# Four small reorderings around a full TensorE: residual copies, a pass change, operand places, and the last stores

## The reference

```python
h = xn @ w_up                       # 1024 -> 2 * 2816
hc = conv_b + sum_j shift(h, j) * conv_w[j]   # causal, 3 taps, per channel
gate, up = split(hc); y = (silu(gate) * up) @ w_down   # 2816 -> 1024
h = h + y
out = h * rsqrt(mean(h * h) + 1e-6) * final_g
```

## Time and profile before

| | |
|---|---|
| median of 3 runs | 1462.41 us (1461.9 to 1462.45) |
| the profiled execution's own time | 1460.3 us |
| its span, first to last instruction | 1458.4 us |
| PE busy | 1443.6 us, 99% |
| DVE busy | 1012.1 us, 69% |
| ACT busy | 700.6 us, 48% |
| POOL busy | 47.4 us, 3% |
| mean granted TensorE clock | 0.998 |

### The profile page before, as it was taken

The page is one execution under the profiler, slowest core; times in us unless marked ns, Lnnn a source line. Parts: engine busy times, 40 slices in busy tenths (PEclk is TensorE's granted clock), DMA queues, the critical chain, the costliest instruction groups (busy, mean ns, idle before and its releaser), DMA issues.

```text
span 1458.4 us, 19919 instructions
## 1 busy us (share of the span) xinstructions
PE 1443.6 (99%) x6983; PEld 1192.4 (82%) x6983; DVE 1012.1 (69%) x1710; ACT 700.6 (48%) x1200; POOL 47.4 (3%) x35
## 2 busy tenths in 40 slices
PE   9999999999999999999999999999999999999997
PEld 7888888888888888888888888888887888888876
DVE  7877667655777734776477776675656888888976
ACT  7655555434444422443475555553344343344665
POOL 0000000002100000000200000000020000000002
PEclk9999999999999999999999999999999999999999
DMA  6222212232322233222432222222333655555554
GB/s 250 87 73 88 87 58 74 87 102 72 130 94 93 79 98 112 101 95 72 131 121 89 86 73 80 65 80 88 122 130 116 206 180 190 211 178 186 203 166 144
DMA packets 49434, 171.38 MB, mean 118 GB/s; under 512 B 6465, under 2 KB 6593, under 8 KB 46289
## 3 DMA queue, kind: packets, MB, share of 16 engines
q1 hardware_dynamic: 45760, 147.43, 30.8%
q10 hardware_dynamic: 3600, 22.99, 4.2%
HBM read 156.70 MB, written 13.63 MB: 117 GB/s over the span
## 4 chain that ended last, share of the span: by engine, by line
PE 93%; DVE 3%; ACT 2%; DMA 1%; issue 1%; POOL 0%; SPq 0%; POOLq 0%; ACTq 0%; DVEq 0%
PE dense L784 26%; PE dense L786 26%; PE dense L785 26%; PE turned L867 2%; PE branch L894 1%; PE dense L799 1%; PE dense L801 1%; PE dense L800 1%; PE dense L1049 1%; PE dense L1051 1%; PE dense L1050 1%; PE scores L859 1%; DMA raw<-in_w_last 1%; PE scores L856 1%; PE branch L880 1%
## 5 line engine op out<-in xcount | busy, mean ns | idle before, releaser
L784 PE MATMUL dense<-hg,whi 128*128 128x512 f32 x1304 | 516.6, 396 | 3.7 <-DVE wlo L1540 3.5
L786 PE MATMUL dense<-hg,wlo 128*128 128x512 f32 x1304 | 508.9, 390 | 0.0
L785 PE MATMUL dense<-hg,whi 128*128 128x512 f32 x1304 | 508.4, 390 | 0.0
L1118 ACT ACTIVATE whi<-raw 128x1024 fp32r<-128x1024 f32 (+3 forms) x242 | 240.8, 995 | 427.2 <-PE dense L786 421.1
L1540 DVE TENSOR_TENSOR wlo<-raw,whi 128x1024 fp32r<-128x1024 f32 (+3 forms) x242 | 276.9, 1144 | 117.0 <-ACT whi L1118 115.0
L784 PEld LDWEIGHTS dense<-hg,whi 128*128 128x128 f32 x1304 | 245.5, 188 | 56.4 <-issue 5.0
L786 PEld LDWEIGHTS dense<-hg,wlo 128*128 128x128 f32 x1304 | 244.9, 188 | 52.1
L785 PEld LDWEIGHTS dense<-hg,whi 128*128 128x128 f32 x1304 | 245.3, 188 | 48.0 <-issue 0.2
L784 PE MATMUL dense<-act,whi 128*128 128x512 f32 x432 | 170.0, 394 | 0.5 <-DVE wlo L1540 0.5
L786 PE MATMUL dense<-act,wlo 128*128 128x512 f32 x432 | 168.4, 390 | 0.0
L785 PE MATMUL dense<-act,whi 128*128 128x512 f32 x432 | 168.3, 390 | 0.0
(11 more groups left out here) (317 smaller groups left out, 1610.5 us busy)
## 6 DMA issues: line engine op xcount, KB each, us to landing
raw<-in_w_up SPq DMA_DIRECT2D x88, 512.0 KB, 3.5
raw<-in_w_gate SPq DMA_DIRECT2D x48, 512.0 KB, 3.5
raw<-in_w_in SPq DMA_DIRECT2D x26, 512.0 KB, 3.5
probT<-in_w_last ACTq DMA_DIRECT2D x10, 1024.0 KB, 6.2
w_sums<-probT ACTq DMA_DIRECT2D x10, 1024.0 KB, 4.3
raw<-in_w_out SPq DMA_DIRECT2D x16, 512.0 KB, 3.5
raw<-in_w_down SPq DMA_DIRECT2D x16, 384.0 KB, 3.0
raw<-w_sums SPq DMA_DIRECT2D x8, 768.0 KB, 4.9
```

Source lines behind the costliest of these rows:

```text
L784: mm(out, a, xhi, start=start, stop=False)
L785: mm(out, a, xlo, start=False, stop=False)
L786: return mm(out, b, xhi, start=False, stop=stop)
L1118: fn(whi[:, s, 0:cols], raw[:, r, 0:cols], ACT.Copy).then_inc(w_hi.sem, 1)
```

## The change

ScalarE's residual copies move behind the third up pair; the fold of `u` on VectorE moves from the end of round 11's low parts to between its second and third; from round 16 on the split operands take three places in turn instead of two; and the end has a new order: reciprocals apart from the output scaling, tile 0's left half scaled and stored by ScalarE instead of POOL and SP, and SP's six stores in the order of a list.

```diff
+RING = KP + 5                       # KP is 11, so RING is 16
 def slot_of(q):
-    return 2 if q == 2 * KP - 1 else q % 2
+    return q % 2 if q < RING else (q - RING + 2) % 3
+OUT_ORDER = ((2, 1, 1), (2, 0, 1), (3, 1, 2), (0, 1, 3), (3, 0, 2), (1, 1, 4))
...
 # SP: stores
-            for i, t in enumerate(LAST_ORDER):
-                for half in range(1 if i == T - 1 else 0, 2):
-                    sp.wait_ge(o_fin_v if half else o_fin_p, i + 1)
-                    sp.dma_start(A["out"][0, t * P:(t + 1) * P, half * S:(half + 1) * S],
-                                 out_st[:, t, half * S:(half + 1) * S]).then_inc(stored, 16)
+            for t, half, count in OUT_ORDER:
+                sp.wait_ge(o_fin_v if half else o_fin_p, count)
+                sp.dma_start(...)
...
 # ACT: last_hi
-                if q_ == 2 * KP - 1:
-                    act.wait_ge(last_l, split_at(KP + 4, "x2"))
+                if q_ == RING:
+                    act.wait_ge(last_l, split_at(RING - 1, "x2"))
                 elif q_ >= 2:
-                    x = {...}[what] if q_ < KP else order_of(q_ - 2)[-1]
-                    act.wait_ge(last_p, product_at(q_ - 2, x))
+                    before = q_ - 2 if q_ < RING else q_ - 3
+                    x = {...}[what] if q_ < KP else order_of(before)[-1]
+                    act.wait_ge(last_p, product_at(before, x))
...
 # ACT: the last layer's up pairs
                     if l == L - 1:
-                        residual_in()
                         act.wait_ge(ssum_done.sem, ssum_done.at(l, C - 1))
                         load_staged(1)
                         up_pair(l, half, 2, 0, True)
+                        residual_in()
                         up_pair(l, half, 3, 1, True, 1)
...
 # ACT: end
-            act.wait_ge(fin_rec, T)
             act.wait_ge(fin_yg, 2)
-            fn(out_st[:, 1, 0:S], y_gained[1], ACT.Copy, scale=stat[:, 1, 1:2]).then_inc(o_fin_a, 1)
-            act.wait_ge(o_fin_a, 1)
-            act.dma_start(A["out"][0, P:2 * P, 0:S], out_st[:, 1, 0:S]).then_inc(stored, 16)
+            for i, t in enumerate((1, 0)):
+                act.wait_ge(fin_rec, T)
+                fn(out_st[:, t, 0:S], y_gained[t], ACT.Copy, scale=stat[:, 1, t:t + 1]).then_inc(o_fin_a, 1)
+                act.wait_ge(o_fin_a, i + 1)
+                act.dma_start(A["out"][0, t * P:(t + 1) * P, 0:S], out_st[:, t, 0:S]).then_inc(stored, 16)
...
 # DVE: down_last
                         last_lo(q_, what)
+                        if (q_, what) == (KP, "x01"):
+                            fold_in("u", 0)
+                            fold_in("u", 1)
                     if q_ == KP:
-                        for x, t in FOLDS:
-                            fold_in(x, t)
+                        fold_in("v", 0)
+                        fold_in("v", 1)
...
 # DVE: end; the reciprocal leaves final_out and becomes reciprocal_of
+            reciprocal_of(0, 2)
             final_out(0, 2)
             bias_of(1, 3)
             gain_left(2, 0)
             bias_of(2, 0)
+            reciprocal_of(1, 3)
+            bias_of(3, 1)
+            gain_left(3, 1)
             final_out(1, 3)
-            gain_left(3, 1)
-            bias_of(3, 1)
+            reciprocal_of(2, 0)
             final_out(2, 0)
+            reciprocal_of(3, 1)
             final_out(3, 1)
...
 # POOL: end
-            for i, t in enumerate(LAST_ORDER[0:3]):
+            for i, t in enumerate(LAST_ORDER[0:2]):
```

More of the change, by code:

```diff
@@ L761, in _ @@
                     load_next_first(l)
-            for i, t in enumerate(LAST_ORDER):
-                for half in range(1 if i == T - 1 else 0, 2):
-                    sp.wait_ge(o_fin_v if half else o_fin_p, i + 1)
-                    sp.dma_start(A["out"][0, t * P:(t + 1) * P, half * S:(half + 1) * S],
-                                 out_st[:, t, half * S:(half + 1) * S]).then_inc(stored, 16)
+            for t, half, count in OUT_ORDER:
+                sp.wait_ge(o_fin_v if half else o_fin_p, count)
+                sp.dma_start(A["out"][0, t * P:(t + 1) * P, half * S:(half + 1) * S],
+                             out_st[:, t, half * S:(half + 1) * S]).then_inc(stored, 16)
             sp.wait_ge(stored, 2 * T * 16)
@@ L1339, in last_hi @@
                 s, r = q_ % 2, raw_last[q_ % 3]
-                if q_ == 2 * KP - 1:
-                    act.wait_ge(last_l, split_at(KP + 4, "x2"))
+                if q_ == RING:
+                    act.wait_ge(last_l, split_at(RING - 1, "x2"))
                 elif q_ >= 2:
-                    x = {"w01": "p5", "x01": "p6", "x2": "p5", "w23": "p4", "x3": "p4"}[what] if q_ < KP else order_of(q_ - 2)[-1]
-                    act.wait_ge(last_p, product_at(q_ - 2, x))
+                    before = q_ - 2 if q_ < RING else q_ - 3
+                    x = {"w01": "p5", "x01": "p6", "x2": "p5", "w23": "p4", "x3": "p4"}[what] if q_ < KP else order_of(before)[-1]
+                    act.wait_ge(last_p, product_at(before, x))
                 elif what[0] == "w":
@@ L2087, in bias_of, with reciprocal_of, final_out @@
                 ve.tensor_scalar(sums[:, t:t + 1], mx[:, t:t + 1], 1.0 / D, eps, ALU.mult, ALU.add).then_inc(fin_bias, 1)
-            def final_out(i, t):
+            def reciprocal_of(i, t):
                 dve.wait_ge(fin_root, i + 1)
                 ve.reciprocal(stat[:, 1, t:t + 1], stat[:, 0, t:t + 1]).then_inc(fin_rec, 1)
+            def final_out(i, t):
                 dve.wait_ge(fin_rec, i + 1)
@@ L2140, in _ @@
             pool.wait_ge(gain_row_in, 16)
-            for i, t in enumerate(LAST_ORDER[0:3]):
[L2142 to L2147, removed]
+            for i, t in enumerate(LAST_ORDER[0:2]):
+                pool.wait_ge(fold, FOLD_AT[("c21", t - 2)])
+                nc.gpsimd.tensor_tensor(y_gained[t], y_left[t], gain_row[:, 0:S], ALU.mult).then_inc(fin_yp, 1)
+                pool.wait_ge(fin_yp, i + 1)
                 pool.wait_ge(fin_rec, i + 1)
```

## The result

The changed kernel takes 1453.57 us (median of 4 runs, 1453.17 to 1453.92), the kernel before 1462.43 us (4 runs, 1461.9 to 1463.2): a ratio of 0.9939, 95% interval 0.9922 to 0.9956. Forecast were 1456.1 us and a range of 1454.7 to 1458.9. The direction was right; the gain is 8.9 us where 6.3 were forecast, and the time lies 1.1 us under the range. The measured interval of the ratio allows gains from 6.4 to 11.4 us, so 6.3 lies just outside it.

A forecast was written before the change was run, and what follows sets the result against it. TensorE was taken as the bound, busy 99% of the span, leaving its waits and a 7.9 us tail to gain. 3.7 + 1.2 + 1.5, taken as 6.3, off 1462.41 gave 1456.1 us, range 1454.7 to 1458.9.

The forecast's parts named there:

- Part 1: Third up pair: with the residual copies moved later, its first matmul follows the transposes sooner, gain 3.7 us.
- the paragraph on the clock: Up product stall: full clock after 3.46 us without a matmul in the trace, so gain 3.7 us alone, no surcharge.
- The step from the profiled execution to the median: Whole kernel: the median stands 2.1 us above the profiled execution, so the gain was subtracted from 1462.41 us.
- Part 2: Pass change, rounds 11 to 13: earlier folds on VectorE remove PE's direct wait and round 12's delay, gain 1.2 us.
- Part 3: Rounds 16 to 21: three operand places let round 21's splits start earlier, gain 0.5 us on PE.
- rival (c): Rounds 16 to 21: three places gain nothing because raw weights land late; 1456.9 us, chance 0.09.
- rival (d): Rounds 16 to 21: loads bunch, land later and hold ScalarE, costing 7.8 us; 1463.9 us, chance 0.03.
- Part 4: Kernel end: new order of scalings and stores, gain 1.5 us including PE's half microsecond from the operand places.
- Rival (a): Kernel end: only PE's half microsecond is gained, as ScalarE's two last activations and issues end late; 1457.0 us, chance 0.12.
- Rival (b): Up product: the 3.5 us stall moves, PE still waits 2 to 3.7 us; 1459.7 us, chance 0.09.

The follow-up runs named there:

- part 1 alone: The kernel before with only the residual copies moved behind the third up pair's high parts: 1456.48 us, ratio 0.9963.
- part 1 undone: The changed kernel with the residual copies moved back to their old place: 1459.06 us.

## Why the prediction was wrong

- **Part 1, 3.7 us.** On TensorE's side the trace is as forecast to 0.1 us: the pair 0.79 us behind the transposes, the next low parts in time. (The staged load was not issued behind the silu but 9 us earlier than before, and so the high part came some half a microsecond sooner than forecast; nothing hung on it.) In the medians part 1 is worth 5.7 us (alone) or 5.5 (undone). This is the term that was mis-sized, and the failing step is the paragraph on the clock. It held the Trainium skill's rule (TensorE: Matmul & The Clock Gate, "What's actually happening") against one trace, found the clock at 1.00 behind the pause, and let the row decide for all executions. The row was right for its execution, and that execution was one of the cheap ones. It also priced the rule too high, at the whole time that matmuls run at the other level: at half pace half of that time is lost, 2.6 us of the 5.3 in the costliest trace (1122.92 to 1128.20). Measured, the loss is 0 to 2.6 us from one execution to the next, and 1.7 (pause filled) to 2.0 (part 1 alone) in the median. No chance was given to this case.
- **The step from the profiled execution to the median.** The prediction noted that the median stands 2.1 us above the profiled execution and carried that over unchanged. It was no constant: to within a few tenths it was the cost of the clock's fall, which the change removes. The changed kernel's offset is 0.4. The 2.1 us were on the page before the forecast, and a difference of this size, where the three timed runs lay within 0.6 us of each other, needed a cause.
- **Part 2, 1.2 us.** Right: 1.25 between the traces (1407.58 - 1118.74 against 1413.12 - 1123.03), 1.1 between the traces when undone.
- **Part 3, 0.5 us on PE.** Right: 0.54. The splits of round 21 ended before they were needed, rival (c) fell, and of rival (d), the loads that bunch, there is no sign: no wait of PE appears in rounds 16 to 21.
- **Part 4, 1.0 us in the tail with part 3's earlier folds.** Right in sum: 6.9 us instead of 7.9. Undoing the order alone costs 0.8 of it. POOL ended 1.7 us earlier against the last matmul (3.9 us behind its start before, 2.2 after), not 2.5; the forecast had counted PE's own half microsecond in, and POOL's scaling took 1.94 instead of 1.7. The output of tile 3 took 0.74 us and not the 1.27 that was taken as likelier. In the new order it starts when POOL's product of two SBUF tensors is all but over (it ends at 1444.22, the output starts at 1444.09), and only POOL's scaling runs beside it; that this is the reason is read from the traces, where it is so every time, and was not tested by itself. Rival (a) fell.
- **Rival (b)**, the stall that moves, fell: PE has no wait left in the up product; the only one on a low part, 0.5 us, is at 1068, in the mixer, and was there before.

The terms by the medians are 5.7 + 1.1 + 1.1 + 0.9 = 8.8 us against 8.9 measured. That it fits to 0.1 us is in part luck: the medians come from different occasions, and parts 3 and 4 share part of the tail. By the traces the last three are 1.1 + 0.7 + 0.8 = 2.6 us, close to the forecast's 2.7. Two slips in the forecast's arithmetic changed nothing: 3.68 + 1.18 + 1.5 is 6.4 and not 6.3, and 1455.1 less half a microsecond is 1454.6 and not 1454.7.

## What to carry to other kernels

A pause of TensorE can cost more than its length: read its price from several executions, because the clock can stay up in one and fall in the next. When the profiled execution stands apart from the timed ones, ask first what varies, and look at each run's mean granted clock; a change that removes the cause takes that difference with it. Where the pause itself cannot be removed, small matmuls into a spare bank can remove the surcharge: here 20 of them, 1.7 us in the median.

## What the runs showed of the hardware

- The same pause of 3.46 us was followed by no slow matmul in two traces of before, by 6 and 12 matmuls at half pace (0.43 us apart instead of 0.23) in two others, and by 8, after five fast ones, in the kernel with part 1 undone. The clock had already fallen within the pause in the costly one (0.80 over 1120.0 to 1122.5) and fell 1.3 us after the pause's end in the last. With the pause filled down to 1.07 us, by matmuls on zeros, it stayed at 1.00.
- VectorE's output from `rel` and the gain row, both in SBUF, took 1.27 and 1.26 us where it ran against POOL's product of two SBUF tensors, and 0.74 and 0.75 us against POOL's scaling of one. POOL's scaling took 2.04 and 1.94 us where such an output was still running for its first 0.60 and 0.51 us, and 3.42 for two in a row where it was for 0.45: less that overlap it is 1.44, 1.43 and 1.49 each, so POOL seems to wait for VectorE's output, an estimate from these rows that no run tested.
- The last six stores of 256 KB, issued within some 3 us, moved at 373 to 387 GB/s together (changed kernel, 1447 to 1450); with the last one issued 0.4 us sooner against the last matmul, the span ended no sooner.
